# A second Strassen group in the down projection of four feed-forward blocks, interleaved with the last up pieces

## The reference, cut to what matters

```python
def swiglu(x, w_gate, w_up, w_down):
    return (jax.nn.silu(x @ w_gate) * (x @ w_up)) @ w_down

x = x + 0.5 * swiglu(rmsnorm(x, ffn1_norm[l]), ffn1_w_gate[l], ffn1_w_up[l], ffn1_w_down[l])
```

## Time and profile before

| | us |
|---|---|
| median of 3 runs (1334.8 to 1335.16) | 1335.14 |
| profiled execution, whole | 1334.76 |
| its span, first to last instruction | 1333.0 |
| PE busy | 1324.6 (99%) |
| DVE busy | 822.4 (62%) |
| ACT busy | 789.8 (59%) |
| POOL busy | 494.1 (37%) |

### The profile page before, as it was taken

How to read it: one execution, slowest core, us unless ns; L and a number is a source line. 1 busy time by engine, 2 the same in 40 slices (tenths; PEclk the granted TensorE clock), 3 DMA queues, 4 the chain that set the end, 5 groups by cost and what they waited for, 6 DMA issues and landing times.

```text
span 1333.0 us, 18862 instructions
## 1 busy us (share of the span) xinstructions
PE 1324.6 (99%) x7312; PEld 1119.5 (84%) x7312; DVE 822.4 (62%) x1066; ACT 789.8 (59%) x1083; POOL 494.1 (37%) x204
## 2 busy tenths in 40 slices
PE   9999999999999999999999999999999999999998
PEld 8888888888888888888888877788888888888887
DVE  6657856945556875557856659754335642555776
ACT  7655467456555566555557697577434655655553
POOL 1463023474547104463023321035525524445500
PEclk9999999999999999999999999999999999999999
DMA  9656864234655785555865655355854443655483
GB/s 347 224 188 211 240 240 156 96 121 151 217 187 185 178 303 194 189 189 156 247 234 178 229 179 196 112 178 175 296 175 176 175 172 128 205 186 182 169 228 119
DMA packets 41114, 256.91 MB, mean 193 GB/s; under 512 B 6192, under 2 KB 6736, under 8 KB 12112
## 3 DMA queue, kind: packets, MB, share of 16 engines
q1 hardware_dynamic: 36832, 230.89, 49.6%
q0 software_dynamic: 2304, 16.78, 6.8%
q10 hardware_dynamic: 1904, 8.23, 1.7%
HBM read 254.80 MB, written 1.08 MB: 192 GB/s over the span
## 4 chain that ended last, share of the span: by engine, by line
PE 95%; DVE 2%; ACT 2%; issue 1%; DMA 0%; POOLq 0%; POOL 0%; ACTq 0%; SPq 0%; DVEq 0%
PE acc L376 20%; PE acc L361 14%; PE acc L363 14%; PE acc L362 14%; PE acc L377 12%; PE acc L379 3%; PE acc L2820 2%; PE work L1171 1%; PE acc L2821 1%; PE acc L618 1%; PE acc L619 1%; PE acc L617 1%; PE work L618 1%; PE work L617 1%; PE work L619 1%; PE work L1256 1%
## 5 line engine op out<-in xcount | busy, mean ns | idle before, releaser
L342 POOL TENSOR_TENSOR wlo<-raw,whi 128x2048 fp32r<-128x2048 f32 x80 | 381.9, 4774 | 492.7 <-ACT whi L337 485.1
L337 ACT ACTIVATE whi<-raw 128x2048 fp32r<-128x2048 f32 (+1 forms) x237 | 438.8, 1858 | 100.1 <-PE acc L363 45.6
L342 DVE TENSOR_TENSOR wlo<-raw,whi 128x2048 fp32r<-128x2048 f32 (+1 forms) x157 | 359.7, 2295 | 172.1 <-ACT whi L337 171.7
L376 PE MATMUL acc<-xT,whi 128*128 128x512 f32 x1208 | 428.0, 396 | 0.2
L377 PE MATMUL acc<-xT,wlo 128*128 128x256 f32 x1384 | 373.6, 280 | 0.0
L376 PEld LDWEIGHTS acc<-xT,whi 128*128 128x128 f32 x1208 | 226.5, 188 | 51.8 <-DVE work L839 1.8
L377 PEld LDWEIGHTS acc<-xT,wlo 128*128 128x128 f32 x1384 | 261.2, 189 | 7.0
L361 PE MATMUL acc<-whi,xT 128*128 128x512 f32 x416 | 168.4, 405 | 0.0
L363 PE MATMUL acc<-whi,xT 128*128 128x512 f32 x416 | 162.5, 391 | 0.0
L362 PE MATMUL acc<-wlo,xT 128*128 128x512 f32 x416 | 162.3, 390 | 0.0
L839 DVE TENSOR_TENSOR work<-acc,low_parts 128x512 f32<-128x512 f32 x88 | 61.5, 698 | 84.6 <-ACT low_parts L721 82.6
(11 more groups left out here) (436 smaller groups left out, 1923.1 us busy)
## 6 DMA issues: line engine op xcount, KB each, us to landing
raw<-in_t_ffn_up SPq DMA_DIRECT2D x85, 1024.0 KB, 5.0
raw<-in_t_m_in SPq DMA_DIRECT2D x52, 1024.0 KB, 4.9
raw<-in_t_ffn_down SPq DMA_DIRECT2D x32, 1024.0 KB, 5.5
raw<-in_t_ffn_down POOLq DMA_DIRECT2D x16, 1024.0 KB, 8.4
raw<-in_t_ffn_down SPq DMA_DIRECT2D x16, 512.0 KB, 6.6
raw<-in_t_m_os SPq DMA_DIRECT2D x8, 1024.0 KB, 5.0
raw<-in_t_m_out SPq DMA_DIRECT2D x4, 1024.0 KB, 4.9
sum_rows<-row_scratch ACTq DMA_DIRECT2D x4, 1024.0 KB, 4.6
```

The lines of the kernel that those rows point to most:

```text
L337: act.activation(granule(whi, u, i), granule(raw, u, i), ACT.Copy).then_inc(hi_ready, 1)
L342: eng.tensor_tensor(granule(wlo, u, i), granule(raw, u, i), granule(whi, u, i).bitcast(F32), ALU.subtract).then_inc(lo_signal(g)[0], 1)
L376: pe.matmul(to, hi[:, c], both_parts(kt), start=first, stop=False)
```

## The change

The rows 8 to 15 of `w_down` become a second Strassen group. There are now 18 granules of the down projection for 16: 14 products, and four ordinary granules (rows 16 to 19, and 20 and 21, of either half). An FFN has 40 places (0 to 39). The places from 10 on (`LATE`) are: up piece 10; then products 0 to 10 in turn with up pieces 11 to 21 (P4 of the first group at place 11, up 11 at 12, P6 at 13, ... P5 at 23, up 17 at 24, P4 of the second group at 25, up 18 at 26, P6 at 27, ... up 21 at 32); then product, granule, product, granule, product, granule, granule.

- All products go to two banks of their own (`work[:, 2]` and `work[:, 3]`), and each is added to `x`: 12 additions a group, and P3 and P5 no longer accumulate with ordinary granules. The up pieces from 5 on use only two banks of `work`.
- POOL makes `wlo` of places 5, 7, 9, 16, 20, 28 and 32; DVE makes all others, those of the up pieces at even places and at 12, 14, 18, 22, 24, 26 and 30 among them. Eight loads add to a slot for four.
- POOL makes `forms` twice. ACT makes `form_hi` after the work of place 9 and of place 23, DVE `form_lo` ahead of the work of places 10 and 24.
- The loops on PE, ACT, DVE and POOL are written out.
- The first half of `x` for the next block is complete after place 36, and is transposed after place 37.

```diff
-        with pe.Fori(0, TURNS) as it:
-            up(3, it)
-            up(4, it)
...
+        for n, entry in LATE.items():
+            u, i = place(f, n)
+            if entry[0] == "up":
+                up(entry[1])
+            elif entry[0] == "product":
...
+                if name == "P6":
+                    pe.wait_ge(forms_split, 2 * (2 * f + group + 1))
+                if k >= 2:
+                    pe.wait_ge(products_added, products_so_far(f, group, name) - 2)
+                multiply_form(pe, u, group, name)
...
+        hi(8)
+        for n in range(5, LAST_UNIT):
+            entry = LATE.get(n, ("up", n))
+            if entry[0] == "up":
+                low(entry[1])
+                hi(n + 4)
+                silu(entry[1])
+                round_hidden(entry[1])
+            elif n < LAST_UNIT - 1:
+                hi(n + 4)
+            if n == 9:
+                round_forms(0)
+            if n == 23:
+                act.wait_ge(gran_done, place_done(f, n))
+                round_forms(1)
...
+        for n in range(5, PLACES):
+            entry = LATE.get(n, ("up", n))
+            if n in (10, 24):
+                rest_forms((10, 24).index(n))
+            if entry[0] == "up":
+                m = entry[1]
+                join(m)
+                row(m)
+                lo(n + 3)
+                product(m)
+                rest_hidden(m)
+            elif entry[0] == "product":
+                if n < 35:
+                    lo(n + 3)
...
+                add_product(n, *entry[1:])
...
+        lo(9)
...
+        make_forms(0)
+        add_to_slot(15)
+        add_to_slot(17)
+        lo(16)
+        add_to_slot(19)
+        lo(20)
+        add_to_slot(23)
+        make_forms(1)
+        add_to_slot(29)
+        lo(28)
+        add_to_slot(31)
+        add_to_slot(33)
+        lo(32)
+        add_to_slot(37)
```

## The result

The changed kernel takes **1425.97 us** (median of 4 runs, 1425.43 to 1426.59) where the kernel before takes 1335.04 (4 runs, 1334.8 to 1335.16): a ratio of 1.0682, 95% interval 1.0663 to 1.07. It is slower by 91 us, 20 more than forecast and above the range's end of 1422.

What follows compares the result with a forecast made beforehand. PE bounds the kernel, with DVE and POOL sharing a port becoming the bound in parts: 20.5 us of waits less 2.7 saved, net 17.8 an FFN, 71 in four, so 1334.8 + 71 = 1406 us; range 1370 to 1422.

Steps and rivals of the forecast that it cites:

- What bounds the kernel, and the 10.9 us to gain: Whole kernel: PE, busy 99%, bounds it; 12 fewer matmuls an FFN save 2.7 us, 10.9 in all four.
- The loops at nothing: Written-out loops on the engines: some register instructions go from queues with room, costed at nothing either way.
- The port: Late up pieces: DVE operations with both inputs in SBUF and POOL's exclude each other; 15 to 24 us an FFN, chance 0.70.
- extra 3.7 us: DVE's additions to x: if they also need the port, 3.7 us more for the FFN.
- The waits: PE's waits in an FFN: 6.9 + 2.2 + 11.1 + 0.3 = 20.5 us, against 2.7 saved.
- The wait at place 14: First group: PE waits 0.8 us for wlo of place 14, which ends after the rest of piece 10.
- the place-27 wait: Second group: PE waits 11.1 us for DVE's wlo of place 27, behind forms, form_lo and POOL's wlo of 28.
- I take it to stay: Granted clock of PE: full in every slice before, assumed to stay full despite long waits, with no time added.
- the term for place 23's load: Places 16 to 26: adding load issued after POOL's wlo of 20, landing 8.4 to 9.5 us later; PE waits 0.5 at 23.
- rival "adding loads": Later adding loads of a group: slower landing brings up to 2.3 us each, some 10 an FFN, 1445 us; chance 0.06.
- 4.6 us less an FFN: Second group's wait of 11.1 us: 4.6 less if the adding load comes in time.
- The chance of slower, 0.88: Whole kernel: chance 0.88 that the change measures slower, against 0.08 for faster by more than 0.2%.

Runs made afterwards that it cites:

- last version: version b with POOL taking place 39 of the second FFN after the gained x, and the 17 small parameter loads spread over places 10 to 18: 1331.63 us, ratio 0.998.
- The run's 6.0: Changed kernel with place 23's adding load issued before POOL splits place 20, and each group's first sum made after four hidden rows: 1401.89 us, 24.1 less, 6.0 an FFN.
- version b: Changed kernel with queues and products reordered, early first sums, forms rounded and split later, POOL splitting places 21, 24, 35 and 39: 1340.13 us, ratio 1.0042.

## Why the prediction was wrong

The last version has nearly no waits, so its dates serve as the row to count from. Starts of products on PE in FFN 0, and the waits that the prediction had summed up to there:

| product at place | changed kernel | last version | later by | foreseen |
|---|---|---|---|---|
| 13 | 80.49 | 77.87 | 2.6 | 2.8 |
| 15 | 92.81 | 87.19 | 5.6 | 6.9 |
| 17 | 102.88 | 95.69 | 7.2 | 6.9 |
| 23 | 130.41 | 120.81 | 9.6 | 7.4 |
| 27 | 159.15 | 137.55 | 21.6 | 20.2 |
| 33 | 187.18 | 163.38 | 23.8 | 20.2 |
| back half of `x` added | 213.24 | 189.18 | 24.1 | 20.5 |

(The last version itself waits 0.78 us at place 15, is about 1 us late from there and 0.7 us more from place 31 on, so the changed kernel is later by that much more than the column "later by" says.)

- **What bounds the kernel, and the 10.9 us to gain:** right. The best version gets 3.3 of them.
- **The loops at nothing:** right, 1.0003.
- **The port:** right in its mechanism and its lengths: 6.60 and 5.63 us for DVE's `wlo`, 4.71 and 6.68 of idle time ahead of `form_lo`. Taking POOL's reads away in the forms gave back 30 us, taking its late `wlo` away 50 together with the earlier load. The extra 3.7 us that the text put on DVE's additions to `x` did not come: all 96 take 0.74 or 0.75 us, those beside POOL's forms too.
- **The waits:** 2.26, 2.27, 2.26, 10.23 and 1.08 in FFN 0 make 18.1 against 20.5 foreseen, and the place-27 wait 10.1 to 10.4 in all four FFNs against 11.1. The wait at place 14 did not come, and one of 1.1 at place 32 of FFN 0 did, which the sum did not have. So the waits were not put too low.
- **The step that failed** in the sum of PE's time is the last paragraph's "I take it to stay" about the clock, a term put at nothing. Waits of 2.3 us came with a granted clock of half, which cost 6.3 us of PE's time in FFN 0 and 23.9 in all. PE's time grew by 73.8 us of idle, 23.9 of slow work and 3.8 that are there at the full clock too, less the 10.9 saved: 90.6, the growth of the span. The forecast had 82, none and none. As a cause of the time the clock is less: with it kept full at place 27 the kernel is 4.4 us faster, and at 13, 15 and 23 nothing comes of it.
- **A second step, mis-sized, is the term for place 23's load.** It took the 8.4 to 9.5 us to landing of the earlier trace rows; this load takes 12.4 to 13.0 to its `whi`. The rival "adding loads" named that, from about 10 us, at 0.06; in the changed kernel one load an FFN does it, not each of the later ones. The sum put the hidden row at 9.9 us behind the end of place 20; POOL's forms start 12.0 behind it in FFN 0 (131.58 - 119.62) and 11.3 to 12.0 in the others. So the row is 1.4 to 2.1 us an FFN late. The text had 4.6 us less an FFN for a load in time. The run's 6.0 are not the answer to that, as they hold the early first sum; the row itself came 3.2 to 4.3 us earlier there, counted from the end of place 20. The mechanism, late load to `whi` to ACT's queue to `rest_hidden` to forms, was the right one.
- **The chance of slower, 0.88,** was on the right side; the range's upper end came from port waits alone, with the unknowns, clock and landing, taken as the rows of before had them.

How the 20 us divide between load, clock and the rest stays open: 4.4 are shown for the clock, the load has a date that is late by 1.4 to 2.1 us an FFN and no run of its own, and the two sums above, by PE's time and by dates, count the same microseconds in two ways.

## What to carry to other kernels

When a change makes PE wait where it never did, its lower clock belongs in the sum, but it only costs where the next wait does not swallow it; the dates of the other engines decide. A late operand is paid for less at the place that needs it than behind the in-order queues that stood for it: follow it through each queue to the next long chain. And a change whose added work fits can still lose 7% by its order: of 91 us here, 85 came back from moving the same instructions, some of them to another engine, and with either of two parts of that move put back 52 and 80 were lost again. And where a wait goes that the moved line cannot reach, as the one at place 13 did here, something else in the kernel differs too.

## What of the hardware was not expected

- PE's granted clock was 0.57 in the 4 us from 80.00 on, behind a wait of 2.26 us, where it had worked at full clock from 70 to 78. It stayed full behind waits of 0.75 us (the run with the load first) and 1.57 us (version b), but also behind 2.14, 2.17 and 2.23 us in the changed kernel and behind 2.54 and 2.86 us in FFN 0 of the run with the products in another order (1.00 in the 4 us from 200 and from 184 on). So the length of a wait alone does not tell; what else decides is not shown.
- An adding load of 1 MB takes 8.6 us in the median and up to 13.0; the one of place 23 in FFN 0 with 12.7 to its `whi` ran beside three plain loads issued within 7 us of it. The Trainium skill, "DMA: Bandwidth & Descriptors", section "Anatomy of one DMA — SWDGE (gpsimd) path", fits 2.0 us and the bytes at 436 GB/s, an estimate of 4.4 us for 1 MB; no adding load in the traces is under 7.8, and the measurement decides.
- The port is as exclusive for DVE's multiplications of `x` as for its `wlo`: 3.81 us for 1.41. Memsets of POOL leave DVE alone: 2.28 us for a `wlo` beside them. POOL does not slow the additions to `x` either, which have one input in PSUM: 0.74 or 0.75 us each, all 96, beside POOL or not.
